# Main products stream the two halves of a moving tile column by column in turn; the banks are read back with a step of two

## The reference, cut to what matters

```
u = h @ w_in                       # first layer: 1024 x 3072
r = sigmoid(block_diag_linear(xc, wa, ba)); i = sigmoid(block_diag_linear(xc, wx, bx))
x = x + (hs * silu(gate)) @ w_out
u = h @ w_in                       # second layer: q, k, v, gate, 1024 x 4112
x = x + (attention(q, k, v, cumulated log_sigmoid) * silu(gate)) @ w_out
for i in range(2):                 # hybrid layers
    cb, cc, cu, q, k, v, g, ga, gb = split(rmsnorm(x) @ w_in)
    o = retention(rotary(q), rotary(k), v)         # 4 heads of 128, values of 256
    merged = sigmoid(ga) * (cb * conv(cc * cu) @ w_conv_out) + sigmoid(gb) * ((silu(g) * norm(o)) @ w_ret_out)
    x = x + merged @ w_o
    x = x + square(relu(rmsnorm(x) @ w_up)) @ w_down
out = rmsnorm(x)
```

## Time and profile before

| | |
|---|---|
| runs | 2256.77, 2257.03, 2257.32 us; median 2257.03 |
| the profiled execution | 2257.17 us, of which the span from the first to the last instruction is 2255.4 |
| PE, PEld busy | 2236.2 and 1837.5 us (99% and 81%) |
| DVE, ACT busy | 1299.6 and 836.4 us (58% and 37%) |
| TensorE's granted clock, mean | 0.997 of full speed |
| read from and written to HBM | 208.14 and 2.10 MB |

### The profile page before, as it was taken

How to read it: one execution, slowest core, us unless ns; L and a number is a source line. 1 busy time by engine, 2 the same in 40 slices (tenths; PEclk the granted TensorE clock), 3 DMA queues, 4 the chain that set the end, 5 groups by cost and what they waited for, 6 DMA issues and landing times.

```text
span 2255.4 us, 27883 instructions
## 1 busy us (share of the span) xinstructions
PE 2236.2 (99%) x10180; PEld 1837.5 (81%) x10190; DVE 1299.6 (58%) x1866; ACT 836.4 (37%) x1162; POOL 1.4 (0%) x6
## 2 busy tenths in 40 slices
PE   9999999999999999999999999999999999999998
PEld 7788878778888888888888888888888888888886
DVE  8878785768555544656444455655435555553545
ACT  6676473635343213234222223333212233222222
POOL 0000000000000000000000000000000000000000
PEclk9999999999999999999999999999999999999998
DMA  5233212123222223222332322222232232223222
GB/s 182 94 103 105 89 51 93 57 80 101 87 93 76 95 92 102 98 98 89 100 101 85 106 99 94 75 94 75 94 103 93 95 100 94 94 93 103 96 100 75
DMA packets 59511, 211.67 MB, mean 94 GB/s; under 512 B 6736, under 2 KB 7120, under 8 KB 59280
## 3 DMA queue, kind: packets, MB, share of 16 engines
q1 hardware_dynamic: 59040, 208.83, 28.1%
q0 software_dynamic: 224, 1.31, 0.2%
q10 hardware_dynamic: 144, 0.12, 0.0%
HBM read 208.14 MB, written 2.10 MB: 93 GB/s over the span
## 4 chain that ended last, share of the span: by engine, by line
PE 84%; DVE 2%; ACT 2%; issue 1%; DVEq 0%; ACTq 0%
PE bank L660 25%; PE bank L662 25%; PE bank L661 25%; PE bank L655 2%; PE bank L657 2%; PE bank L656 2%; PE bank L840 1%; PE bank L890 1%; PE bank L832 1%; ACT arena L1205 0%; ACT arena L1143 0%; PE bank L813 0%; PE bank L918 0%; PE bank L814 0%; DVE y_lo L1679 0%
## 5 line engine op out<-in xcount | busy, mean ns | idle before, releaser
L1369 DVE TENSOR_TENSOR w_lo<-w_raw,w_hi 128x1024 fp32r<-128x1024 f32 x387 | 467.5, 1224 | 748.7 <-ACT w_hi L989 747.6
L989 ACT ACTIVATE w_hi<-w_raw 128x1024 fp32r<-128x1024 f32 x387 | 404.1, 1057 | 921.7 <-PE bank L662 881.0
L660 PE MATMUL bank<-h_hi,w_hi 128*128 128x512 f32 x1788 | 699.9, 391 | 4.9 <-DVE arena L1404 1.9
L662 PE MATMUL bank<-h_hi,w_lo 128*128 128x512 f32 x1788 | 695.9, 389 | 0.0
L661 PE MATMUL bank<-h_lo,w_hi 128*128 128x512 f32 x1788 | 695.7, 389 | 0.0
L660 PE MATMUL bank<-y_hi,w_hi 128*128 128x512 f32 x1048 | 408.5, 390 | 1.6 <-DVE w_lo L1369 1.3
L661 PE MATMUL bank<-y_lo,w_hi 128*128 128x512 f32 x1048 | 407.7, 389 | 0.0
L662 PE MATMUL bank<-y_hi,w_lo 128*128 128x512 f32 x1048 | 407.7, 389 | 0.0
L660 PEld LDWEIGHTS bank<-h_hi,w_hi 128*128 128x128 f32 x1788 | 335.6, 188 | 77.9 <-DVE w_lo L1369 4.8
L661 PEld LDWEIGHTS bank<-h_lo,w_hi 128*128 128x128 f32 x1788 | 335.7, 188 | 70.4 <-issue 1.4
L662 PEld LDWEIGHTS bank<-h_hi,w_lo 128*128 128x128 f32 x1788 | 335.6, 188 | 70.3
(11 more groups left out here) (236 smaller groups left out, 1496.4 us busy)
## 6 DMA issues: line engine op xcount, KB each, us to landing
w_raw<-in_stream SPq DMA_DIRECT2D x389, 512.0 KB, 3.3
x<-in_x_t SPq DMA_DIRECT2D x8, 256.0 KB, 6.7
out_t<-x SPq DMA_DIRECT2D x8, 256.0 KB, 2.2
arena<-in_consts POOLq DMA_DIRECT2D x1, 1024.0 KB, 5.1
w_raw<-in_stream SPq DMA_DIRECT2D x2, 256.0 KB, 4.3
arena<-in_positions POOLq DMA_DIRECT2D x1, 256.0 KB, 6.2
vec_t<-in_vecs ACTq DMA_DIRECT2D x1, 112.5 KB, 3.2
ident<-in_consts SPq DMA_DIRECT2D x1, 64.0 KB, 6.7
```

Of the source, the lines that this page charges most:

```text
L660: pe.matmul(out, w_hi[:, slot, w], a_h, start=first, stop=False)
L662: mm = pe.matmul(out, w_lo[:, slot, w], a_h, start=False, stop=last)
L989: A.activation(w_hi[:, slot, :], w_raw[:, slot, :], ACT.Copy).then_inc(hi_ready, 1)
L1369: V.tensor_tensor(w_lo[:, slot, :], w_raw[:, slot, :], w_hi[:, slot, :].bitcast(F32), ALU.subtract).then_inc(lo_ready, 1)
```

## The change

`streamed` gives the columns of a tile in the order 0, 256, 1, 257, and so on: a step of half the tile from each column to the next. Every float32r matmul of the main products takes its moving operand through it, so column 2i of a bank belongs to token i and column 2i + 1 to token 256 + i. The matmuls still write their bank in unbroken order. `in_order` reads such a bank back as two runs of 256 columns, each with a step of two columns; `halves` shapes the other operand and the result alike, so that everything in SBUF stays as it was. For the step `v`, where the weights move, the stream is stored with its even and odd columns apart, so that the bank comes out in order and its readers are not changed. The statistics of `ret_out` (`bn_stats`, line 1854) still read their bank in unbroken order, since they do not depend on it. The number and order of instructions, the waits and the transfers are the same on every engine.

```diff
+        def streamed(row):
+            return row.rearrange("p (a b) -> p b a", a=2)
+        def in_order(row):
+            return row.rearrange("p (b a) -> p a b", a=2)
+        def halves(row):
+            return row.rearrange("p (a b) -> p a b", a=2)
...
-                                pe.matmul(out, a_h[:, t], w_hi[:, slot, w], start=first, stop=False)
-                                pe.matmul(out, a_h[:, t], w_lo[:, slot, w], start=False, stop=False)
-                                mm = pe.matmul(out, a_l[:, t], w_hi[:, slot, w], start=False, stop=last)
+                                w_h, w_l = streamed(w_hi[:, slot, w]), streamed(w_lo[:, slot, w])
+                                pe.matmul(out, a_h[:, t], w_h, start=first, stop=False)
+                                pe.matmul(out, a_h[:, t], w_l, start=False, stop=False)
+                                mm = pe.matmul(out, a_l[:, t], w_h, start=False, stop=last)
...
-                                pe.matmul(out, w_hi[:, slot, w], a_h, start=first, stop=False)
-                                pe.matmul(out, w_hi[:, slot, w], a_l, start=False, stop=False)
-                                mm = pe.matmul(out, w_lo[:, slot, w], a_h, start=False, stop=last)
+                                pe.matmul(out, w_hi[:, slot, w], streamed(a_h), start=first, stop=False)
+                                pe.matmul(out, w_hi[:, slot, w], streamed(a_l), start=False, stop=False)
+                                mm = pe.matmul(out, w_lo[:, slot, w], streamed(a_h), start=False, stop=last)
...
-                        pe.matmul(out, st_hi[hh][:, at:at + P], rv_hi[:, j, cols], start=j == 0, stop=False)
-                        pe.matmul(out, st_hi[hh][:, at:at + P], rv_lo[:, j, cols], start=False, stop=False)
-                        mm = pe.matmul(out, st_lo[:, hh, at:at + P], rv_hi[:, j, cols], start=False, stop=j == t)
+                        pe.matmul(out, st_hi[hh][:, at:at + P], streamed(rv_hi[:, j, cols]), start=j == 0, stop=False)
+                        pe.matmul(out, st_hi[hh][:, at:at + P], streamed(rv_lo[:, j, cols]), start=False, stop=False)
+                        mm = pe.matmul(out, st_lo[:, hh, at:at + P], streamed(rv_hi[:, j, cols]), start=False, stop=j == t)
...
+            def product_bank(n):
+                return in_order(the_bank(n)[:, :])
...
-                    V.tensor_tensor(tile(n), the_bank(n)[:, :], rms[:, :], ALU.mult).then_inc(evacuated, 1)
+                    V.tensor_tensor(halves(tile(n)), product_bank(n), halves(rms[:, :]), ALU.mult).then_inc(evacuated, 1)
...
-                    V.tensor_tensor(x[:, 4 * j + n, :], the_bank(n)[:, :], x[:, 4 * j + n, :], ALU.add)\
-                        .then_inc(evacuated, 1)
+                    x_n = halves(x[:, 4 * j + n, :])
+                    V.tensor_tensor(x_n, product_bank(n), x_n, ALU.add).then_inc(evacuated, 1)
...
-                    V.tensor_scalar(st[:, hh, t * RV:t * RV + RV], the_bank(t)[:, 0:RV],
+                    V.tensor_scalar(halves(st[:, hh, t * RV:t * RV + RV]), in_order(the_bank(t)[:, 0:RV]),
...
-                        A.activation(to[:, q, :], bank[set_ + 2 * q + n][:, :], ACT.Sigmoid,
+                        A.activation(halves(to[:, q, :]), in_order(bank[set_ + 2 * q + n][:, :]), ACT.Sigmoid,
...
+    def stored_by_halves(chunks):
+        return chunks.reshape(-1, P, KT, 256, 2).transpose(0, 1, 2, 4, 3).reshape(-1, P, CW)
```

More of the change, by code:

```diff
@@ L673, in bank_by_bank @@
                         w = slice(kt * 512 + n * P, kt * 512 + n * P + P)
-                        pe.matmul(out, w_hi[:, slot, w], a_h, start=False, stop=False)
-                        pe.matmul(out, w_hi[:, slot, w], a_l, start=False, stop=False)
-                        mm = pe.matmul(out, w_lo[:, slot, w], a_h, start=False, stop=kt == KT - 1)
+                        pe.matmul(out, w_hi[:, slot, w], streamed(a_h), start=False, stop=False)
+                        pe.matmul(out, w_hi[:, slot, w], streamed(a_l), start=False, stop=False)
+                        mm = pe.matmul(out, w_lo[:, slot, w], streamed(a_h), start=False, stop=kt == KT - 1)
                     mm.then_inc(bank_ready, 1)
@@ L683, in first_tile @@
                 for n in range(4):
-                    pe.matmul(bank[n][:, :], w_hi[:, 0, n * P:n * P + P], h_hi[:, 0, :], start=True, stop=False)
+                    pe.matmul(bank[n][:, :], w_hi[:, 0, n * P:n * P + P], streamed(h_hi[:, 0, :]), start=True, stop=False)
                 h_ready(0)
                 for n in range(4):
-                    pe.matmul(bank[n][:, :], w_hi[:, 0, n * P:n * P + P], h_lo[:, 0, :], start=False, stop=False)
+                    pe.matmul(bank[n][:, :], w_hi[:, 0, n * P:n * P + P], streamed(h_lo[:, 0, :]), start=False, stop=False)
                 pe.wait_ge(lo_half, 1)
                 for n in range(4):
-                    pe.matmul(bank[n][:, :], w_lo[:, 0, n * P:n * P + P], h_hi[:, 0, :], start=False, stop=False)
+                    pe.matmul(bank[n][:, :], w_lo[:, 0, n * P:n * P + P], streamed(h_hi[:, 0, :]), start=False, stop=False)
             def statistics(set_):
@@ L745, in gates @@
                     y = xc_slot(b, 2 * half + blk)
-                    pe.matmul(bank[set_ + n][:, :], w_hi[:, slot, w], y_hi[:, y, :], start=True, stop=False)
-                    pe.matmul(bank[set_ + n][:, :], w_hi[:, slot, w], y_lo[:, y, :], start=False, stop=False)
-                    pe.matmul(bank[set_ + n][:, :], w_lo[:, slot, w], y_hi[:, y, :], start=False, stop=True)\
+                    pe.matmul(bank[set_ + n][:, :], w_hi[:, slot, w], streamed(y_hi[:, y, :]), start=True, stop=False)
+                    pe.matmul(bank[set_ + n][:, :], w_hi[:, slot, w], streamed(y_lo[:, y, :]), start=False, stop=False)
+                    pe.matmul(bank[set_ + n][:, :], w_lo[:, slot, w], streamed(y_hi[:, y, :]), start=False, stop=True)\
                         .then_inc(bank_ready, 1)
@@ L788, in forget @@
                     out = bank[set_][:, :]
-                    pe.matmul(out, w_hi[:, slot, w], h_hi[:, k, :], start=k == 0, stop=False)
-                    pe.matmul(out, w_hi[:, slot, w], h_lo[:, k, :], start=False, stop=False)
-                    mm = pe.matmul(out, w_lo[:, slot, w], h_hi[:, k, :], start=False, stop=k == DT - 1)
+                    pe.matmul(out, w_hi[:, slot, w], streamed(h_hi[:, k, :]), start=k == 0, stop=False)
+                    pe.matmul(out, w_hi[:, slot, w], streamed(h_lo[:, k, :]), start=False, stop=False)
+                    mm = pe.matmul(out, w_lo[:, slot, w], streamed(h_hi[:, k, :]), start=False, stop=k == DT - 1)
                 mm.then_inc(bank_ready, 4)
@@ L1272, in qk_step @@
                     for a, b in ((0, RQK // 2), (RQK // 2, 0)):
-                        A.activation(swap[a:a + RQK // 2, n % 2, :], bank[set_ + n][b:b + RQK // 2, :],
-                                     ACT.Copy).then_inc(act_out, 1)
+                        A.activation(halves(swap[a:a + RQK // 2, n % 2, :]),
+                                     in_order(bank[set_ + n][b:b + RQK // 2, :]), ACT.Copy).then_inc(act_out, 1)
             def ret_out(step):
@@ L1905, in ret_proj @@
                     banks(n)
-                    m = m_t[:, half * 4 + n, :]
-                    V.tensor_tensor(m, the_bank(n)[:, :], m, ALU.mult).then_inc(evacuated, 1)
+                    m = halves(m_t[:, half * 4 + n, :])
+                    V.tensor_tensor(m, product_bank(n), m, ALU.mult).then_inc(evacuated, 1)
                 if step.args.get("rescale"):
@@ L1924, in cu_step @@
                         got(n - 1)
-                    V.tensor_tensor(tmp2[:, n % 2, :], the_bank(n)[:, :], rms[:, :], ALU.mult).then_inc(evacuated, 1)
+                    V.tensor_tensor(halves(tmp2[:, n % 2, :]), product_bank(n), halves(rms[:, :]), ALU.mult)\
+                        .then_inc(evacuated, 1)
                     read(n)
@@ L1967, in merge @@
                     banks(n)
-                    g = ga_t[:, 4 * j + n, :]
-                    V.tensor_tensor(g, the_bank(n)[:, :], g, ALU.mult).then_inc(evacuated, 1)
+                    g = halves(ga_t[:, 4 * j + n, :])
+                    V.tensor_tensor(g, product_bank(n), g, ALU.mult).then_inc(evacuated, 1)
                 for n in range(4):
```

17 lines of the change are left out of this document (11 added, 6 removed).

## The result

| | before | changed |
|---|---|---|
| median of 4 runs, us | 2256.90 (2256.47 to 2257.32) | 2170.47 (2169.16 to 2171.60) |
| span of the profiled execution, us | 2255.4 | 2169.8 |
| ratio of the runs | | 0.9617, 95% interval 0.9600 to 0.9634 |

The change made the kernel 3.8% faster, 86.4 us. I had forecast 4,145 us, in a range from 2,250 to 4,290.

The account below looks back on a forecast made before the run. PE's float32r matmuls were taken to bound the kernel. 2,257 us plus 1,894 for two cycles a column (1,871 and 23), less 6 of covered waits, gave 4,145 us, in a range from 2,250 to 4,290.

Parts of the forecast that it names:

- What bounds the kernel: On PE: 9,216 float32r matmuls of 512 columns, 226.7 ns apart, make 2,089 us, 93% of the span.
- The moving operand: Columns read by PE's main matmuls: without neighbours each takes two cycles, adding 1,894 us in all; chance 0.52.
- the term of 203 ns a matmul: Addition per 512-column float32r matmul at plain float32's two cycles a column (592 - 389 ns); 9,216 of them make 1,871 us.
- The rest: About 13.3 ns per float32r matmul beyond one cycle a column, same at 512 and 256 columns; all that could be won.
- The faster rival: Between float32r matmuls: the 13.3 ns shrinks until steps reach bf16's 216 ns, 99 + 3 us won, 2,155 us; chance 0.10.
- The waits: PE's four waits for the low part of a weight chunk, 6.6 us: longer products cover them, 6 us taken off.
- The readbacks: DVE and ACT reading banks with a step of two: no added cost; upper end 0.54 us a bank, 4.9 us on the path.
- the slow rate of 1.05 ns a column: DVE's column rate from PSUM or SBUF, slower than PE's 0.417 ns; the reason for taking the readbacks' cost as nothing.
- a case that no row of before showed: Main matmuls on PE at two cycles a column, 4,145 us, own range 4,110 to 4,270; chance 0.52.

Follow-up runs that it names:

- the first set: Separate small kernel, 24 matmuls of each moving pattern back to back, nothing of the reference computed: float32r at 512 columns 226.7 ns in order, 215.8 in two runs in turn.
- the third: Further patterns in a separate small matmul-only kernel, among them wider distances, repeated columns and widths 64 to 512: groups of 8 and 16 float32r columns took 243 and 240 ns.

## Why the prediction was wrong

**What bounds the kernel.** Right: 9,216 matmuls that carry 93% of the span set the time, and a change of their step showed in full, less the waits.

**The moving operand, where it failed.** The step was "the change takes away every neighbour. Then a column costs one step more, and two cycles is the only slower step that this trace shows". I took neighbours in the order for neighbours in what the reader fetches. The moving columns alone brought 2,170.04 us, so the term of 203 ns a matmul was -10.9, and that is nearly all of the error. The count that fits many of the runs is another one: even and odd places of the order each want several columns from one group of 16 bytes. In turn, each of them gets four where in order it gets two; by this count the change did not take neighbours away, it doubled them. The bound itself exists: one run with a step of two took 453 ns, four runs in turn 283, and the kernel with four came out at 2,762 us.

**The rest.** "It belongs to the matmul or its weight load, not to a column" was read from two widths, 512 and 256. As a reading it stands for the weight load of the kernel, and a third width agrees (13.3, 13.3 and 13.0 ns at 512, 384 and 256 columns). As an explanation it does not: with a weight load of 32 columns the part that the change removes goes from 1.0 ns at 64 columns to 15.8 at 512. I had the right size, and its end of 216 ns was met exactly, but put the wrong place behind it; so the rival got 0.10.

**The faster rival.** Its size was right (99 + 3 us, measured 102.4), its total of 2,155 off by the 15 us of new waits, and its mechanism not borne out: a smaller weight load takes nothing off the rest, and two runs 4 columns apart are as good as 256. That its number came so near was luck: I borrowed the bf16 step for it without a reason why columns in turn should end there, and they do.

**The waits.** I took 6 us off because slower products would cover them, and gave the faster rival none. The sign is right for slow products (17.2 us before, 7.7 with four runs in turn), and giving the faster rival none was wrong: 16.7 us were added, some of them at half the clock.

**The readbacks.** Right in size: 687 ns, and 2257.17 us with them alone. The reason that I gave, the slow rate of 1.05 ns a column, was not tested.

**The rule on lines.** The Trainium skill (SBUF — State Buffer, the cachelines under "Door 1: The DMA port swizzle"; Advanced Engine Details and Errata, "Memory Cachelines") asks for two hits on a 16-byte line. By that rule this change had to lose and a float32r step of two to be free; here it won 10.9 ns, and the step of two took 453. Where the Trainium skill and a measurement differ, the measurement decides. The rule holds in spirit, that what shares a line is cheap; its count does not fit PE.

The other rule (the Trainium skill, SBUF — State Buffer, "Who interferes with whom": PE's read ports for moving columns and for weights are independent) said that there was nothing to win. 10.9 ns a matmul were won, on the moving side alone. The weight loads of 64 and 32 columns agree with independent ports, since they took nothing off the step. The stationary operand read with a step of 16, which took the step from 215.8 to 228.0 ns, leaves it open.

**The chances.** 0.52 on a case that no row of before showed, because it was the only other rate in the trace. What the trace did show was a rest of float32r over bf16 at the same width, 10 ns in mean duration: the same columns in half the bytes ran at the full rate, which was a hint that bytes per group are what matters, and I spent it on a rival.

## What to carry to other kernels

Where PE is bound by float32r matmuls, stream the moving columns as two runs in turn, each taking whole groups of four columns and read the bank back to match. With the halves of the tile that is a step of two: 216 ns in place of 227 at 512 columns, and the readback cost nothing here. Runs 4, 8, 16 and more columns apart have the same step, but a readback to match them was not tried. Runs 5 and 3 columns apart took 240 and 269, more than in order. Don't take one run with a step, four runs, or bf16 runs in turn: 453, 283 and 484 ns. And look at the seams afterwards: an engine that gets 5% faster arrives at waits that were hidden, and here two of them, of 3.6 and 3.1 us, were followed by half the clock.

## What I had not expected of the hardware

- The order in which a moving operand is read changes a matmul's step in both directions: 215.8, 226.7, 283 and 453 ns for the same 512 float32r columns. Even and odd places counted apart against 16-byte groups explain many kinds. Left open: groups of float32r columns from two halves (328 ns for groups of 2 in the first set and 340 in the third; 250, 243 and 240 ns at 4, 8 and 16), four and eight runs, steps of 4 columns and more, why bf16 runs in turn take 432 to 484 ns, and why columns in order take between 226.7 and 236.7 ns by where they start. That there are two readers is a model that fits the counts; nothing here shows them.
- Plain float32 is slower in turn too, 540 ns against 428 to 432, while float32r gains.
- The granted clock fell to 0.50 after PE had stood for 3.6 us in the changed kernel, and did not after the same wait in another run. In the first pattern set it also fell while PE was never idle, during the bf16 matmuls with a step of eight columns. Their steps are 900 ns on either side of the fall at 272 us:

```profile
269.00:272.00 3.00, 3.00 (x5) 0.45 (x4) 0.00 (x0) 0.00 (x0) 0.00 (x0) 1.00 0.00 0
272.00:290.00 18.00, 18.00 (x21) 2.61 (x20) 0.00 (x0) 0.00 (x0) 0.00 (x0) 0.50 0.00 0
```
